# A fourth set of 32 tokens takes the way of fetched expert rows, and 384 instead of 416 stay dense

## The chip, the core and the metric

The kernel runs on one core of a Trainium2 chip. Its time is the device time of one launch in microseconds (us). Three runs of the kernel before gave 2327.8, 2332.86 and 2333.51 us; the median is 2332.86.

## What is computed

Two transformer blocks follow one another on 512 tokens of width 1024. The change lies in the last part of the first block, a feed-forward layer of 16384 experts. Every token picks 128 of them (8 heads, 16 each) and gets a gate for each pick:

```python
u_sel = u[expert]          # expert: [tokens, 128] of 16384; u, v: [16384, 1024]
v_sel = v[expert]
act = gelu(einsum('nd,ned->ne', hx, u_sel))
out = einsum('ne,ned->nd', gate * act, v_sel)
```

The sums are carried out in pairs of fp16 halves (a high and a low part), three matmuls for each product.

## The kernel before

**Two ways through the experts.** 416 tokens (`DENSE`) are computed densely: all 16384 experts in 128 chunks (`CHUNKS`) of 128. In the up pass TensorE multiplies each u tile with the tokens (`up`, 8 x 3 matmuls of 416 columns), ScalarE takes the gelu (`gelu_chunk`), and SyncE stores the result to `act_mem` (`store_act`). From chunk 58 (`AT_GATES`) on, one group of 8 tokens a chunk has its gates spread: VectorE builds one-hot rows (`pick`, four instructions), TensorE multiplies them (`spread_gates`, 16 matmuls), ScalarE copies them out (`place_gates`), and after every 13 groups (`BATCH // GROUP`) ScalarE issues one store to `gate_mem`. A batch waits for the store of the batch before the last. In the down pass SyncE loads for each chunk the v tile and the pair of `act_mem` and `gate_mem` (`load_pair`), VectorE multiplies the pair (`multiply`, L2169) and takes its low part (`low_part`, L2174), ScalarE makes the high parts, GpSimd cuts the v tile's low part (`cut_v`, L843), and TensorE does 24 matmuls of 416 columns (`down_chunk`).

**The other 96 tokens** (`FEW`, three sets of 32, `SET`) lie in the last block of 128. The 128 partitions hold a set's 32 tokens in four parts (`SIDES`), each with a quarter of the token's picks, so one fetch brings one row of u or v for each of 128 picks (512 KB), and a set takes 32 fetches of u and 32 of v. GpSimd issues them (`fetch`, L825) into six buffers (`ROWS_AHEAD`). For u, TensorE first puts the set's tokens into two PSUM banks (`turn_few`), and VectorE makes one `dot` for each row (L2013). For v, VectorE adds each row, times its weight, to the set's sum (`add_few`, L2184 and L2186), and TensorE folds the four parts at the end (L1297).

**What sets the order.** All queues are written out by hand. `dots_at` places dots 0 to 51 between the steps of VectorE's top-16 search (`CHOICE`, blocks 3, 0, 1, 2), which lasts until chunk 57 of the up pass; `dots_behind` places the others behind the picks of a group. GpSimd fetches row n before its cut of chunk `row_chunk(n)`, which is `dot_chunk(n - ROWS_AHEAD) + 4`, and waits there until dot n - 6 is done. In the down pass GpSimd and VectorE go by one rule:

```python
def fetch_chunk(k):
    return 112 * k // FEW
# GpSimd: for c in range(CHUNKS): fetch all k with fetch_chunk(k) <= c, each once add k - 6 is done; then cut_v(c)
# VectorE: for c in range(CHUNKS): multiply(c); low_part(c - 1); add all k with fetch_chunk(k) + 2 <= c
# SyncE:   for each c: load v tile c + V_LEAD (5) once cut_v(c + 1) is done; then load_pair(c) once multiply(c - 4) is done
```

The ring of v tiles has 4 places (`RING`), `pair` has 4, and the cut parts have 16. TensorE waits before the down pass until all dots are done, and before its end until all adds are.

Of the kernel before, what the change touches and what calls it, by code (L numbers as in the profile page):

```python
# [47 lines left out]
CHUNKS = 128  # L48
GROUP = 8
SET = 32  # L50
SETS = 3
FEW = SET * SETS
DENSE = S - FEW
BATCH = DENSE // 4
# [9 lines left out]
CHOICE = (3, 0, 1, 2)  # L64
FETCH = AT_ROWS + 7
STEPS = 20
FIRST_DOTS, EARLY_DOTS = 4, 52
STAIR = 65
TAIL = CHUNKS - GROUP
A_H, A_KV, A_G = 16, 4, 4  # L70
# [81 lines left out]
def build(nc, x_in, c_in, vec_in, rows1_in, rows2_in, ple_in, ada_in, w_in, u_in, v_in, u_rows_in, x_park, act_mem,  # L152
# [7 lines left out]
    with ctx:  # L160
# [3 lines left out]
        def sem(name):  # L164
            return ctx.enter_context(nc.semaphore(name))
# [253 lines left out]
        rows_used = sem("expert_rows_used")  # L419
# [52 lines left out]
        per_turn = P // GROUP  # L472

        def gate_chunk(g):

            return AT_GATES + g

        def groups_at(c):
            return [g for g in range(GROUPS) if gate_chunk(g) == c]

        def dots_behind(g):

            return [n for n in range(EARLY_DOTS, FEW)
                    if g == (n - EARLY_DOTS + 1 if n < 2 * SET else n - 2 * SET + 19)]

        def dots_at(at, step):

# [8 lines left out]

        def dot_chunk(n):

            if n >= EARLY_DOTS:
                return gate_chunk([g for g in range(GROUPS) if n in dots_behind(g)][0])  # L500
            return 19 + 7 * n // 10 if n < SET else AT_FEWER + 1 + 11 * (n - SET) // 20

        def row_chunk(n):

            return dot_chunk(n - ROWS_AHEAD) + 4
# [5 lines left out]
        def few_rows(j):  # L511

            return ps[:, 6:8, :].rearrange("p a b -> p (a b)")
# [380 lines left out]
        def _(pe):  # L894
# [11 lines left out]
            def three(out_, lhs, rhs, start, stop):  # L906

                ins = [T.matmul(out_, a, b, start=start and j == 0, stop=stop and j == 2)  # L908
                       for j, (a, b) in enumerate(((lhs[0], rhs[0]), (lhs[0], rhs[1]), (lhs[1], rhs[0])))]
                return ins[0], ins[2]  # L910
# [277 lines left out]
            def up(r, c, it):  # L1188

                pe.wait_ge(parts_ready, c + (T_EXP + 1))  # L1190
                if not (isinstance(c, int) and c < 2):
                    pe.wait_ge(gelu_ready, c - 1)
                for k in range(KC):
                    hi, lo = hr(k)
                    first, last = three(ps[:, r % 2, 0:DENSE], piece(T_EXP + r, k * P, P),
                                        (hi[:, 0:DENSE], lo[:, 0:DENSE]), k == 0, k == KC - 1)
                    if k == 0:
                        first.then_inc(begun, 1)
                last.then_inc(up_ready, 1)

            def spread_gates(r, g, first):

                pe.wait_ge(picked, g + 1)
                for q in range(2):
                    if not first:
                        pe.wait_ge(gates, g * 2 + (q - 1))
                    for t in range(4):
                        tok = q * 4 + t
                        for p in range(2):
                            mm = T.matmul(ps[:, 2 + q, t * P:(t + 1) * P], first_hot[:, r % 2, tok, :],  # L1210
                                          second_hot[:, 2 * (r % 2) + p, tok, :], start=(p == 0), stop=(p == 1))
                    mm.then_inc(gates_sum, 1)
# [9 lines left out]
            def turn_picks(i):  # L1222

                turns[0] += 1
                if i >= 2:
                    pe.wait_ge(picked, per_turn * (i - 1))
                for j in range(3):
                    mm = T.transpose(picks_of(i)[:, j * P:(j + 1) * P], chosen(i)[:, j, :], ident[:, :])
                mm.then_inc(turned, 1)

            def turn_few(j):
                first = DENSE + j * SET
                for k in range(KC):
                    for side in range(SIDES):
                        for h, half in enumerate(hr(k)):
                            mm = T.matmul(few_rows(j)[side * SET:(side + 1) * SET, k * P:(k + 1) * P],
                                          half[:, first:first + SET], ident_h, start=(h == 0), stop=(h == 1))
                mm.then_inc(few_turned, 1)
# [7 lines left out]
            for c in range(AT_FEWER // 4 * 4, CHUNKS):  # L1246
                up(c % 4, c, 0)
                if c == AT_FEWER:
                    pe.wait_ge(rows_used, SET)
                    turn_few(1)  # L1250
                if c == AT_TURN:
                    pe.wait_ge(tok_ready, 10 + NT)
                    turn_picks(0)
                    turn_picks(1)
                for g in groups_at(c):
                    spread_gates(g % 4, g, g == 0)
                    if g in (per_turn + 1, 2 * per_turn + 1):
                        turn_picks(g // per_turn + 1)
                    if g == 16:
                        pe.wait_ge(rows_used, 2 * SET)  # L1260
                        turn_few(2)


            pe.wait_ge(gelu_ready, CHUNKS)
# [26 lines left out]
            for o in range(KC):  # L1291
                for c in range(TAIL, CHUNKS):
                    lhs, rhs = down_parts(c % (2 * GROUP), o)
                    three(ps[:, o, 0:DENSE], lhs, rhs, False, c == CHUNKS - 1)
                for j in range(SETS):
                    at = DENSE + j * SET
# [67 lines left out]
        def _(act):  # L1364
# [45 lines left out]
            def attention(units, u0, parts_of):  # L1410
                def exps_of(u):
                    un = units[u]
                    soft_b, probs_b, _, sm = soft_buffers(un["kind"])
                    w = un["nc"] * P
                    act.wait_ge(max_ready, u0 + u + 1)
                    if u0 + u >= 2:
                        act.wait_ge(probs_turned, u0 + u - 1)
                    src = ps[:, 4 + u % 2, 0:w] if un["kind"] == "latent" else soft_b[:, u % 2, 0:w]
                    own.do(A.activation(probs_b[:, u % 2, 0:w], src, ACT.Exp, bias=peak(un, u),
                                        scale=1.0 if un["kind"] == "latent" else -1.0, accum_out=total(un, u)), probs)  # L1420
                    if un["kind"] == "window" and u % EIGHT == EIGHT - 1:
                        act.wait_ge(sink_shifted, u // EIGHT + 1)
                        own.do(A.activation(eight_sinks(u), eight_sinks(u), ACT.Exp), sink_exps)
# [106 lines left out]
            def bounce_in(j, dst, signal):  # L1530
                for q in range(SIDES):
                    rows = pick_mem[j][:, q * SET:(q + 1) * SET].rearrange("(s t) k -> t s k", s=SETS)
                    act.dma_start(dst[q * SET:(q + 1) * SET, :].rearrange("p (s k) -> p s k", s=SETS),
                                  rows).then_inc(signal, 16)
# [145 lines left out]
        def _(dve):  # L1680
# [322 lines left out]
            def await_rows(n):  # L2003

                dve.wait_ge(rows_fetched[n % ROWS_AHEAD], 16 * (n // ROWS_AHEAD + 1))
                return fetched_rows[:, n % ROWS_AHEAD, :]

            def dot(n):

                if n % SET == 0:  # L2010
                    dve.wait_ge(few_turned, n // SET + 1)
                row = await_rows(n)
                V.tensor_tensor_reduce(out=row, in0=row, in1=few_rows(n // SET), scale=1.0, scalar=0.0,  # L2013
                                       op0=ALU.mult, op1=ALU.add,
                                       accum_out=few_dot[:, n:n + 1]).then_inc(rows_used, 1)
# [101 lines left out]
            def take_picks(i):  # L2117

                turned_n[0] += 1
                dve.wait_ge(turned, turned_n[0])  # L2120
                src = picks_of(i)
                gate = src[:, 2 * P:3 * P].unsqueeze(2).broadcast_to([P, P, 2])
                own.settle()
                own.do(V.tensor_copy(pairs[:, 0:2, :, :].rearrange("p j n t -> p (j n) t"),
                                     src[:, 0:2 * P].unsqueeze(2).broadcast_to([P, 2 * P, 2])))
                own.link(V.tensor_scalar(pairs[:, 2, :, :], gate, GS, None, ALU.mult))
                own.link(V.scalar_tensor_tensor(out=pairs[:, 3, :, :], in0=gate, scalar=GS, in1=pairs[:, 2, :, :],
                                                op0=ALU.mult, op1=ALU.subtract))
                own.link(V.tensor_copy(src, pair_words), turned_read)
# [24 lines left out]
            for g in range(GROUPS):  # L2154
                if g % per_turn == 0:
                    take_picks(g // per_turn)
                pick(g % 2, g // per_turn, g % per_turn, g, g < 2)
                for n in dots_behind(g):
                    dot(n)


            def multiply(at, c, it):
# [260 lines left out]
```

## Time and profile before

| | |
|---|---|
| median of three runs | 2332.86 us |
| the profiled execution | 2325.09 us, its span 2323.1 us |
| TensorE busy | 2160.9 us (93% of the span) |
| VectorE, GpSimd, ScalarE busy | 1576.3, 1497.8, 920.3 us |
| up pass of the experts | about 413 to 1017 us |
| down pass | 1025 to 1577 us |
| mean granted clock of TensorE | 0.979 |
| DMA over the span | 451.55 MB, 194 GB/s |

All times in the rows are us from the span's start. Engine names there: PE is TensorE, DVE VectorE, ACT ScalarE, POOL GpSimd, SP SyncE. L2169 is line 2169 of the kernel.

### The profile page before, as it was taken

The page shows a single profiled execution, that of the slowest core. Times are in us where ns is not written, and L with a number is a line of the kernel's source. Part 1 is how long each engine was busy: PE and PEld are TensorE (multiplying, and loading weights), DVE is VectorE, ACT ScalarE, POOL GpSimd, SP SyncE. Part 2 cuts the span into 40 slices and gives each one's busy share as a digit, 9 for nine tenths or more (in the row PEclk, how much of TensorE's full clock was granted, in tenths as well). Part 3 has the DMA queues.
Part 4 walks back from the last instruction along what each step waited for, and adds up shares of the span by engine and source line. Part 5 has one row for each costly group of instructions (what it writes and reads, how often), then busy time and mean ns, then how long its engine had stood idle before and what let it go on. Part 6 is the DMA issues. An engine that isn't in the chain of part 4 may idle for free. (4 is left out here: it accounts for less than half of the span.)

```text
span 2323.1 us, 36974 instructions
## 1 busy us (share of the span) xinstructions
PE 2160.9 (93%) x12908; PEld 1182.5 (51%) x12908; DVE 1576.3 (68%) x2807; ACT 920.3 (40%) x1606; POOL 1497.8 (64%) x1032
## 2 busy tenths in 40 slices
PE   5998898999989999989999999998988979989897
PEld 2543543555546666545555555553555435446543
DVE  7597866998896677038889888953047454556644
ACT  2211411455556666543333333322156222245522
POOL 6885586768755555467787777753844758733473
PEclk9999998999999999999999999999999999989998
DMA  7333543579978999989999999852300223300031
GB/s 281 101 96 115 187 148 118 159 266 350 333 237 268 290 355 341 286 312 337 332 341 337 329 338 326 286 182 61 113 29 1 89 75 99 93 19 1 13 91 42
DMA packets 218057, 451.55 MB, mean 194 GB/s; under 512 B 83200, under 2 KB 132544, under 8 KB 217920
## 3 DMA queue, kind: packets, MB, share of 16 engines
q1 hardware_dynamic: 119696, 313.67, 39.7%
q0 software_dynamic: 27648, 100.68, 12.2%
q10 hardware_dynamic: 70576, 35.40, 6.2%
q8 instruction: 83, 1.36, 0.2%
q14 instruction: 54, 0.44, 0.1%
HBM read 390.86 MB, written 58.82 MB: 194 GB/s over the span
## 5 line engine op out<-in xcount | busy, mean ns | idle before, releaser
L908 PE MATMUL ps<-hT,parts 128*128 128x416 f16 (+1 forms) x4800 | 932.9, 355 | 30.6 <-POOL parts L811 9.8
L908 PEld LDWEIGHTS ps<-hT,parts 128*128 128x128 f16 x4800 | 467.2, 98 | 475.7 <-issue 21.7
L908 PE MATMUL ps<-arena 128*128 128x416 f16 x3072 | 544.3, 340 | 12.8 <-DVE arena L2174 11.3
L908 PEld LDWEIGHTS ps<-arena 128*128 128x128 f16 x3072 | 300.7, 98 | 254.2 <-issue 15.0
L817 POOL TENSOR_TENSOR parts<-ring,parts 128x1024 f16<-128x1024 f32 x120 | 256.0, 2135 | 198.4 <-ACT ring L1541 197.2
L808 POOL TENSOR_SCALAR parts<-ring 128x1024 f16<-128x1024 f32 x141 | 163.5, 1160 | 240.0 <-PE ps L908 205.7
L811 POOL TENSOR_TENSOR parts<-ring,parts 128x1024 f16<-128x1024 f32 x141 | 309.7, 2196 | 11.8
L843 POOL TENSOR_TENSOR arena<-ring,arena 128x1024 f16<-128x1024 f32 x128 | 293.5, 2303 | 24.9 <-ACT arena L1578 22.9
L2169 DVE TENSOR_TENSOR route<-arena 128x416 f32<-128x416 f32 x128 | 169.9, 1327 | 128.0 <-DMA arena<-gate_mem 125.1
L1375 ACT ACTIVATE arena<-ps 128x512 f32<-128x512 f32 (+9 forms) x266 | 135.9, 532 | 246.8 <-PE ps L908 141.7
L908 PE MATMUL ps<-arena,parts 128*128 128x512 f16 x876 | 193.5, 381 | 11.6 <-POOL parts L811 5.8
L1593 ACT ACTIVATE arena<-route 128x416 f16<-128x416 f32 x128 | 70.3, 549 | 318.5 <-DVE route L2169 318.5
L2186 DVE SCALAR_TENSOR_TENSOR hT<-arena,spare,hT 128x1024 f32<-128x1024 f32 x93 | 193.9, 2085 | 0.0
L825 POOL DMA_INDIRECT arena<-v,spare x96 | 108.6, 1131 | 97.0 <-DVE hT L2186 84.8
L852 POOL TENSOR_SCALAR arena<-arena 128x512 f16<-128x512 f32 (+3 forms) x80 | 43.9, 549 | 191.0 <-ACT arena L1375 191.0
L1520 ACT ACTIVATE spare<-ps 128x416 f32<-128x416 f32 x128 | 66.3, 518 | 251.2 <-PE ps L908 249.2
L809 POOL TENSOR_SCALAR ring<-ring 128x1024 f32<-128x1024 f32 x141 | 161.3, 1144 | 0.0
L908 PEld LDWEIGHTS ps<-arena,parts 128*128 128x128 f16 x876 | 85.4, 98 | 119.4 <-issue 12.6
L1578 ACT ACTIVATE arena<-ring 128x1024 f16<-128x1024 f32 x128 | 133.2, 1041 | 11.8 <-DMA ring<-v 11.8
L1540 ACT ACTIVATE parts<-ring 128x1024 f16<-128x1024 f32 x120 | 125.8, 1048 | 2.7 <-DVE xT L2108 2.7
L2013 DVE CUSTOM_DVE_ANT_0 arena<-arena,ps 128x1024 f32<-128x1024 f32 x96 | 115.9, 1216 | 14.7 <-DMA arena<-u_rows,spare 8.4
L1541 ACT ACTIVATE ring<-ring 128x1024 f32<-128x1024 f32 x120 | 125.6, 1046 | 0.0
(223 smaller groups left out, 2628.4 us busy)
## 6 DMA issues: line engine op xcount, KB each, us to landing
ring<-w SPq DMA_DIRECT2D x133, 512.0 KB, 3.6
ring<-u SPq DMA_DIRECT2D x128, 512.0 KB, 6.2
ring<-v SPq DMA_DIRECT2D x128, 512.0 KB, 4.6
act_mem<-spare SPq DMA_DIRECT2D x128, 208.0 KB, 5.1
gate_mem<-arena ACTq DMA_DIRECT2D x4, 6656.0 KB, 51.4
arena<-act_mem SPq DMA_DIRECT2D x128, 208.0 KB, 4.2
arena<-gate_mem SPq DMA_DIRECT2D x128, 208.0 KB, 5.5
arena<-ada_w SPq DMA_DIRECT2D x48, 512.0 KB, 5.3
```

What stands on the lines that cost most here:

```text
L808: G.tensor_scalar(dst[:, 0, :], src, WS, 1.0, ALU.mult, ALU.mult).then_inc(scaled, 1)
L809: G.tensor_scalar(src, src, WS, 1.0, ALU.mult, ALU.mult).then_inc(scaled, 1)
L811: G.tensor_tensor(dst[:, 1, :], src, dst[:, 0, :], ALU.subtract).then_inc(parts_ready, 1)
L817: G.tensor_tensor(dst[:, 1, :], src, dst[:, 0, :], ALU.subtract).then_inc(parts_ready, 1)
L843: G.tensor_tensor(dst[:, 1, :], src, dst[:, 0, :], ALU.subtract).then_inc(parts_ready, 1)
L908: ins = [T.matmul(out_, a, b, start=start and j == 0, stop=stop and j == 2) for j, (a, b) in enumerate(((lhs[0], rhs[0]), (lhs[0], rhs[1]) ...
L1375: return A.activation(dst, src, ACT.Copy, scale=scale)
L1540: A.activation(parts[:, n % RING, 0, :], src, ACT.Copy, scale=WS).then_inc(raised, 1)
L1541: A.activation(src, src, ACT.Copy, scale=WS).then_inc(raised, 1)
L1578: A.activation(v_parts[:, c % (2 * GROUP), 0, :], ring[:, (S_V + c) % RING, :], ACT.Copy).then_inc(v_high, 1)
L2169: V.tensor_tensor(prod[:, at % 2, :], pair[:, at % 4, 0, :], pair[:, at % 4, 1, :], ALU.mult).then_inc(product, 1)
L2186: V.scalar_tensor_tensor(out=sums, in0=row, scalar=w, in1=sums, op0=ALU.mult, op1=ALU.add).then_inc(rows_used, 1)
```

## The change

The number of sets goes from 3 to 4, so 128 tokens (the whole last block) go by fetched rows and 384 stay dense. All sizes that hang on it follow: matmuls, gelus, multiplies and stores have 384 columns, there are 48 groups of gates instead of 52 in batches of 12 instead of 13 groups, 128 fetches, dots and adds instead of 96 on each side, and `fetch_chunk` spreads 128 fetches over the same 112 chunks. The third set's dots stand behind the gates of groups 18 to 46. The dots of the fourth set come on VectorE after the last group; TensorE turns that set's tokens after chunk 108 (`AT_LAST`), and for the fetches its dots count two to a chunk from chunk 109.

```diff
-SETS = 3
+SETS = 4
-FIRST_DOTS, EARLY_DOTS = 4, 52
+FIRST_DOTS, EARLY_DOTS, AT_LAST = 4, 52, 108
@@ dots_behind
             return [n for n in range(EARLY_DOTS, FEW)
-                    if g == (n - EARLY_DOTS + 1 if n < 2 * SET else n - 2 * SET + 19)]
+                    if g == (n - EARLY_DOTS + 1 if n < 2 * SET else 18 + 29 * (n - 2 * SET) // SET) and n < 3 * SET]
@@ dot_chunk
+            if n >= 3 * SET:
+                return AT_LAST + 1 + (n - 3 * SET) // 2
@@ TensorE, up pass
-                    if g in (per_turn + 1, 2 * per_turn + 1):
+                    if g == per_turn + 1:
                         turn_picks(g // per_turn + 1)
                     if g == 16:
                         pe.wait_ge(rows_used, 2 * SET)
                         turn_few(2)
+                if c == AT_LAST:
+                    pe.wait_ge(rows_used, 3 * SET)
+                    turn_few(3)
@@ VectorE, after the groups
+            for n in range(3 * SET, FEW):
+                dot(n)
```

## Rows read from the trace of the kernel before

**Rows 1.** Windows: engine busy (instructions), then granted clock, DMA share, GB/s.

```profile
820.00:880.00 60.00, 60.00 (x475) 38.29 (x474) 44.99 (x74) 38.90 (x58) 36.49 (x24) 1.00 1.08 355
...
1200.00:1400.00 200.00, 200.00 (x1139) 111.29 (x1138) 181.10 (x138) 71.85 (x96) 155.38 (x89) 1.00 0.93 332
```

**Rows 2.** Timeline of one chunk with gates: start, us, engine, line.

```profile
858.91 4.38 PE L908 MATMUL ps<-hT,parts 128*128 128x416 f16 x24
...
859.11 0.69 DVE L2146 TENSOR_TENSOR xT<-xT,ps 128x1024 f16<-128x1024 f16 x1 [1.30 <-PE ps L1210]
...
861.70 1.21 DVE L2013 CUSTOM_DVE_ANT_0 arena<-arena,ps 128x1024 f32<-128x1024 f32 x1
...
864.02 4.38 PE L908 MATMUL ps<-hT,parts 128*128 128x416 f16 x24
```

**Rows 3.** Timeline of TensorE before the gates: turn_few, and the wait of chunk 57.

```profile
481.06 1.09 PE L1236 MATMUL ps<-xT,hT 128*32 128x128 f16 x64
...
670.75 1.54 PE L1228 MATMUL ps<-ident,arena 128*128 128x128 f32 x6 [2.88 <-DVE xT L2108]
```

**Rows 4.** Pieces of the chain that ended last, in the down pass.

```profile
1373.94 2.14 POOL arena L843
...
1377.26 6.24 DMA arena<-gate_mem
...
1389.07 0.76 issue
1389.82 1.02 POOL arena L825
```

**Rows 5.** Waits from 1040 to 1500 us: total, times, longest.

```profile
POOL arena L825 <- DVE hT L2186: 84.8, 37, 3.0
```

**Rows 6.** Timeline of VectorE in the down pass.

```profile
1301.46 0.58 DVE L2169 TENSOR_TENSOR route<-arena 128x416 f32<-128x416 f32 x1
...
1302.46 1.27 DVE L2186 SCALAR_TENSOR_TENSOR hT<-arena,spare,hT 128x1024 f32<-128x1024 f32 x1
...
1304.66 3.15 DVE L2186 SCALAR_TENSOR_TENSOR hT<-arena,spare,hT 128x1024 f32<-128x1024 f32 x1
...
1333.94 3.15 DVE L2186 SCALAR_TENSOR_TENSOR hT<-arena,spare,hT 128x1024 f32<-128x1024 f32 x1
```

**Rows 7.** Waits from 480 to 640 us, VectorE's.

```profile
DVE arena L2013 <- DMA arena<-u_rows,spare: 8.4, 10, 1.7
DVE arena L2013 <- PE ps L1236: 5.9, 1, 5.9
```

**Rows 8.** The four gate stores (L1571): time to landing.

```profile
DMA to landing us min/median/max: 43.5/51.4/61.9
```

**Rows 9.** Timeline of GpSimd with two fetches a chunk.

```profile
611.40 0.95 POOL L825 DMA_INDIRECT arena<-u_rows,spare  x1
...
615.91 0.95 POOL L825 DMA_INDIRECT arena<-u_rows,spare  x1 [0.16 <-issue]
```

**Rows 10.** Timeline of the down pass: start, chunk 3, no gap from 1064.55, end.

```profile
1025.28 10.41 PE L908 MATMUL ps<-arena 128*128 128x416 f16 x48 [8.44 <-DVE arena L2174]
...
1032.39 2.51 DVE L2169 TENSOR_TENSOR route<-arena 128x416 f32<-128x416 f32 x1
...
1064.55 473.09 PE L908 MATMUL ps<-arena 128*128 128x416 f16 x2688 [1.05 <-DVE arena L2174]
...
1567.69 4.38 PE L908 MATMUL ps<-arena 128*128 128x416 f16 x24
...
1572.50 4.38 PE L908 MATMUL ps<-arena 128*128 128x416 f16 x24
```

**Rows 11.** The gate half of the pair (L756): time to landing.

```profile
DMA to landing us min/median/max: 2.6/5.5/7.9
```

**Rows 12.** DMA issues from 1503 to 1532 us, where no rows are fetched.

```profile
arena<-gate_mem SPq DMA_DIRECT2D x11, 208.0 KB, 4.4
```

**Rows 13.** Windows behind the change of pass, columns as in rows 1.

```profile
1020.00:1030.00 10.00, 4.72 (x17) 2.23 (x18) 6.40 (x4) 1.89 (x3) 4.89 (x4) 0.66 1.03 411
```

## The prediction

> **What bounds the kernel now.** I read the windows first, to see which engine has no gaps in which stage. In the second half of the experts (the "down" pass) TensorE is busy all the time: 1139 matmuls in 200 us, 0.1756 us each, so a chunk of 24 takes 4.21 us [rows 1]. That is 416 columns at the granted clock of 1.00 with about 2.4 ns on top, so with 384 columns a matmul takes 0.1625 us and a chunk 3.90 us. In the "up" pass a chunk that also spreads gates takes 5.11 us between two starts of its matmuls [rows 2], so TensorE sets the pace there too. Read no further, and the change gives 0.31 us on each of 256 chunks.
>
> But TensorE is not alone. Before chunk 57 it waits for VectorE's gates [rows 3]. And in the down pass the chain of waits runs for long stretches not through TensorE but round a loop [rows 4]: VectorE adds a fetched row; 0.80 us later GpSimd issues the next fetch (1.02 us), then cuts a v tile (2.14 us); SyncE then issues that tile's successor and, behind it, the pair of act_mem and gate_mem (1.18 us from the cut's end to the gate issue); the pair lands 6.24 us later; then VectorE can multiply. GpSimd waited for VectorE's adds 84.8 us in 37 places [rows 5]. The reader is to see that this loop is near the bound before anything is changed: VectorE's seven chunks take 1333.94 - 1304.66 = 29.28 us against TensorE's 7 x 4.21 = 29.5 [rows 6].
>
> **The up pass.** (1) Chunks 0 to 57. VectorE sets the end. Its own waits there are 8.4 us for rows whose fetch is paced by TensorE's chunks, and 5.9 for turn_few(1) at chunk 43, which comes 44 x 0.31 = 13.8 us earlier [rows 7]. Together 14.3 can go, no more, though TensorE saves 18; I take -13, and keep -6 if rows are just as late. (2) Gates: 52 x 5.11 = 265.7 becomes 48 x (5.11 - 0.31) = 230.4, -35.3. Chunks without gates: 18 x 4.21 = 75.8 becomes 22 x 3.90 = 85.8, +10. turn_few(3) is 64 matmuls, which took 1.09 us before [rows 3], +1.1. The picks on VectorE (four fewer) and its 32 more dots of 1.3 us lie beside TensorE: a chunk of 4.80 holds 2.6 of picks and 1.3 of dot [rows 2], and they cost nothing until they pass 4.80. (3) The gate stores: one takes 43.5 to 61.9 us [rows 8], and the batch after next waits for it. A batch now lasts 12 x 4.80 = 57.6 us instead of 66.4, with more rows fetched beside it, so the one at 61.9 is late: +4 (0 to 8). (4) The last set. Rows 102 to 127 are fetched two to a chunk. Where the kernel does that now, GpSimd needs 615.91 - 611.40 = 4.51 us a chunk for two issues and a cut [rows 9], against TensorE's 3.90: 13 x 0.61 = 7.9, less some 3 of lead. The last gate store runs beside; the DMA engines are at 355 GB/s in the window where a store and one row a chunk meet [rows 1]. Two a chunk and the store ask for more. I take +8 (3 to 18). ScalarE's larger pick transfers are hidden: pick_row is ready before chunk 12. Sum of the up pass: -13 - 35.3 + 10 + 1.1 + 4 + 8 = -25 (-38 to -8). The change of pass, 8.44 us of waiting now [rows 10], has 6 row fetches behind the last dots: +2 (0 to 8).
>
> **The down pass, where it is decided.** Rows ahead are 6, and k's fetch stands before chunk fc(k) = 112k//FEW on GpSimd, its add in chunk fc(k)+2 on VectorE. Fetch k waits for add k-6. With FEW = 96, fc(k-6) = fc(k) - 7, so the cut of chunk c waits for VectorE's chunk c-5. With FEW = 128 six rows are only 5.25 chunks: the cut of c waits for VectorE's chunk c-3, and for c-4 in one of seven. The pair of chunk c is issued behind the cut of c+1. Write M(c) for the multiply's start, A(c) for the end of that chunk's adds, K for the way from an add to the multiply. Now M(c) >= A(c-4) + K; after, M(c) >= A(c-2) + K, and A(c-3) + K in one of seven. All that waits behind GpSimd's fetch is late with it: the cut, SyncE's v load, and behind that the pair.
>
> K from the chain [rows 4]: 0.80 + 1.02 + 2.16 + 1.18 + landing. The gate piece's landing is 6.24 in the chain, 5.5 in the median, 2.6 at the least, and 4.4 where no rows are fetched (1503 to 1532 us) [rows 11, 12]. The traffic will be slower than now, since the loop itself is; I take 5.0, so K = 10.2, and keep 4.4 and 6.24 (9.6 and 11.4). A(c) - M(c) is three instructions of VectorE, 1.00 for the two short ones and 1.2 [rows 6], 2.2 us (384 columns save 0.03 on each of two), and 3.4 where two rows are added.
>
> The lags repeat every seven chunks, and the dearest way round goes 5, 2, 0 and back to 5: steps of 3, 2 and 2 chunks. So seven chunks take at least 3K + 2.2 + 2.2 + 3.4 = 30.6 + 7.8 = 38.4 us. After the chunk with two adds GpSimd still has the cut before to finish when its row is free, 2.2 more (0 to 2.2): 40.6, or 5.8 a chunk, against TensorE's 27.3. The low end is 28.8 + 7.8 = 36.6, the high one 34.2 + 10 = 44.2.
>
> Now from chunk 3's multiply at 1032.39 to the last fold at 1577.3 is 545 us [rows 10]. After: chunks 3 to 9 some 30 us, then 105 chunks, 15 x 40.6 = 609, then TensorE alone: 15 x 3.90 = 58.5, one us before it, and eight folds of 0.8 instead of 0.6 (four sets instead of three): 66. Sum 705, +160.
>
> Total: -25 + 2 + 160 = +137. The profiled execution took 2325.1 (span 2323.1), so 2462 against its own time; it lies below all three runs, 7.8 under their median of 2332.9, and I set the sum on the median: 2470. The runs spread over 5.7 us, so 0.3%, 7 us, is about what this measurement can tell from no change.
>
> **Rivals.**
> *Only the shared access bounds.* VectorE's adds and multiplies and GpSimd's cuts take turns: an add that takes 1.27 alone takes 3.15 beside a cut [rows 6]. Seven chunks are 7 cuts of 2.14 [rows 4] and 14 x 0.5 + 6 x 1.2 = 14.2, in all 29.2, near the 29.28 found. After: 15.0 + 6.5 + 9.6 + 0.1 = 31.2, below 40.6. Were the window of rows no bound, the down pass would be 30 + 15 x 31.2 + 66 = 564, +19, and the whole -4: 2329. For it: the sum fits so well. Against: it leaves K out, which the chain shows. 0.07.
> *Short landings.* All pairs land in the 2.6 us of the least row: K = 7.8, cycle 23.4 + 10 = 33.4, down 597, +52, whole +29: 2362. Against: the median is 5.5. 0.06. The Trainium skill, DMA: Bandwidth & Descriptors, "Anatomy of one DMA", gives 2.0 us plus the bytes over 436 GB/s for a GpSimd-issued transfer; for 197 KB that would be an estimate of 2.45 us, and the whole would be about +24. The trace's median of 5.5, issued by SyncE behind a v tile, speaks against it.
> *TensorE stays the bound (faster).* Then the down pass gives 128 x 0.31 = 40 back, less 1.6 of folds: -61, 2272. It needs K + 2.2 <= 2 x 3.90, so K below 5.6, of which 5.2 is spent before the landing. For it: TensorE has no gap now from 1064.55 on [rows 10]. 0.04.
> *TensorE's clock.* It will be idle a third of each down chunk. After the 8.44 us of waiting its granted clock was 0.66 over 10 us in which it was busy for 4.7; in the 200 us with no gap it was 1.00 [rows 1, 13]. At its lower level, 1.2 GHz, a chunk is 7.7 us: were it there all the time, +197 on top. But it would then be busy throughout and climb again. 0.03, over 2535. The Trainium skill, TensorE: Matmul & The Clock Gate, Part 1, says an idle array falls to the half clock; whether gaps this short do it, no row of this stage shows.
>
> **How the numbers follow.** The forecast has 0.80. Its own range is 2398 (cycle 36.6, -60, and up pass -13 more) to 2535 (cycle 44.2, +54, and up +17 more, not both in full). The 80% range is the same, 2395 to 2535; it leaves out the cases at 2272, 2329, 2362 and the clock, 0.2. Faster by over 0.3%: the 0.04 and a third of the 0.07; same: another third; slower: the rest, 0.91.
>
> **What would show it.** In the profile after: chunks of 3.90 in the up pass; chunk 57 waiting longer for VectorE; seven down chunks in 37 to 44 us on VectorE; TensorE at 65 to 70% there; waits of VectorE for gate_mem several hundred us in total, in nearly each chunk; GpSimd waiting for VectorE's adds in nearly each; GB/s near 260 instead of 332. The prediction is wrong if GpSimd's fetches seldom wait for adds, or if landings are near 2.6 us.

## The result and the profile after

The changed kernel takes 2539.41 us (median of 4 runs, 2535.31 to 2542.95) against 2333.19 for the kernel before (4 runs, 2327.8 to 2334.63): a ratio of 1.0886, 95% interval 1.0866 to 1.0907, so 8.9% slower. The forecast was 2470 and the range 2395 to 2535; the direction and the stage were as forecast, the size was not: the result lies 4 us above the range. The profiled execution has a span of 2537.1 us, 214.0 more than before. The page's part 1 now gives TensorE 2155.8 us busy, 85% of the span, VectorE 1513.0, GpSimd 1545.7; the mean granted clock is 0.946.

In the kernel after, L910 is the dense matmul, L2176 the multiply, L2181 the low part, L2191 and L2193 the adds, L827 the fetch, L845 the cut of a v tile, L693, L757 and L758 SyncE's issues of the v tile, act_mem and gate_mem.

The windows that answer to [rows 1], and the whole down pass (columns as there):

```profile
820.00:880.00 60.00, 60.00 (x508) 40.73 (x507) 47.19 (x78) 42.29 (x63) 39.23 (x27) 1.00 1.08 379
1060.00:1750.00 690.00, 501.52 (x2688) 275.90 (x2688) 343.25 (x357) 169.40 (x232) 382.96 (x233) 0.90 0.73 243
1200.00:1400.00 200.00, 140.27 (x757) 76.26 (x758) 105.55 (x103) 48.52 (x66) 105.86 (x69) 0.92 0.74 244
```

With gates TensorE still has no gap. In the down pass it does 757 matmuls in 200 us where it did 1139; no engine is near full, and the DMA engines moved 244 GB/s where they moved 332.

TensorE's timeline at the first gates, near the end of the up pass, and at the change of pass:

```profile
659.13 1.17 PE L1230 MATMUL ps<-ident,arena 128*128 128x128 f32 x6 [3.19 <-DVE xT L2113]
...
671.11 4.06 PE L910 MATMUL ps<-hT,parts 128*128 128x384 f16 x24
...
675.90 4.06 PE L910 MATMUL ps<-hT,parts 128*128 128x384 f16 x24
...
942.01 4.07 PE L910 MATMUL ps<-hT,parts 128*128 128x384 f16 x24 [0.77 <-POOL parts L819]
946.53 4.07 PE L910 MATMUL ps<-hT,parts 128*128 128x384 f16 x24 [0.44 <-POOL parts L819]
...
1004.53 9.52 PE L910 MATMUL ps<-arena 128*128 128x384 f16 x48 [18.80 <-DVE arena L2181]
```

A chunk with gates is 675.90 - 671.11 = 4.79 us (5.11 before, [rows 2]), one with two fetches 946.53 - 942.01 = 4.52. The up pass ends at 1004.53 - 18.80 = 985.73; before it was 1025.28 - 8.44 = 1016.84 [rows 10]. So the up pass gave 31.1 us, and the wait behind it took back 10.4. ScalarE's timeline says what was late there:

```profile
992.34 2.00 ACT L1583 ACTIVATE arena<-ring 128x1024 f16<-128x1024 f32 x2 [8.89 <-DMA gate_mem<-arena]
```

That is the last gate store. The trace's rows of gate_mem (the four stores, and the landing of all transfers with that name):

```profile
L1576 ACTq DMA_DIRECT2D gate_mem<-arena x4: 378/393/437, 721.7 to 895.7; - x4
...
DMA to landing us min/median/max: 2.5/5.0/96.5
```

Issued at 895.7, it landed 96.5 us later, at 992.2; before, the longest took 61.9 [rows 8]. It shares the DMA engines with two row fetches a chunk: from 935 to 955 us they moved 409 GB/s at a share of 1.04. SyncE's queue holds the first pairs behind this store, and behind the pairs a store of act_mem, for which ScalarE's last gelu waited another 8.35 us, until 1002.69. From the first down matmul to chunk 3's multiply is 7.8 us (7.1 before); from there to the last fold 779.2 us (544.9). So -31.1 + 10.4 + 0.7 + 234.3 = +214.3, the whole difference of the spans. TensorE's timeline of the end of the down pass and VectorE's of its chunk 3:

```profile
1752.30 5.49 PE L910 MATMUL ps<-arena 128*128 128x384 f16 x24 [6.65 <-POOL parts L813]
...
1790.61 0.97 PE L1302 MATMUL ps<-spare,hT 128*128 128x32 f32 x8
```

```profile
1012.36 0.55 DVE L2176 TENSOR_TENSOR route<-arena 128x384 f32<-128x384 f32 x1
```

The waits from 1010 to 1750 us (total, times, longest), the answer to [rows 5], and the issue line of the pair's gate half with its median landing in us, to [rows 11]:

```profile
DVE route L2176 <- DMA arena<-gate_mem: 365.6, 78, 10.7
POOL arena L827 <- DVE hT L2193: 276.4, 70, 7.4
PE ps L910 <- DVE arena L2181: 200.0, 66, 7.8
```

```profile
arena<-gate_mem SPq DMA_DIRECT2D x124, 192.0 KB, 5.0
```

Each engine of the loop waits for the next one round: VectorE for the pair, GpSimd for VectorE's add; TensorE, which is not in the loop, waits for VectorE. That is the loop of the prediction, and the median landing is the 5.0 us taken there.

One turn of it on VectorE, on GpSimd, and the first issues on SyncE's queue:

```profile
1409.25 1.28 DVE L2193 SCALAR_TENSOR_TENSOR hT<-arena,spare,hT 128x1024 f32<-128x1024 f32 x1
...
1411.51 4.34 DVE L2193 SCALAR_TENSOR_TENSOR hT<-arena,spare,hT 128x1024 f32<-128x1024 f32 x2
1422.04 0.56 DVE L2176 TENSOR_TENSOR route<-arena 128x384 f32<-128x384 f32 x1 [6.19 <-DMA arena<-gate_mem]
...
1426.86 0.56 DVE L2176 TENSOR_TENSOR route<-arena 128x384 f32<-128x384 f32 x1 [2.60 <-DMA arena<-gate_mem]
...
1439.63 0.56 DVE L2176 TENSOR_TENSOR route<-arena 128x384 f32<-128x384 f32 x1 [8.28 <-DMA arena<-gate_mem]
...
1453.12 0.56 DVE L2176 TENSOR_TENSOR route<-arena 128x384 f32<-128x384 f32 x1 [8.98 <-DMA arena<-gate_mem]
```

```profile
1411.34 1.08 POOL L827 DMA_INDIRECT arena<-v,spare  x1 [6.22 <-DVE hT L2193]
1412.44 2.33 POOL L845 TENSOR_TENSOR arena<-ring,arena 128x1024 f16<-128x1024 f32 x1
1414.92 1.76 POOL L827 DMA_INDIRECT arena<-v,spare  x1 [0.15 <-issue]
1416.70 2.13 POOL L845 TENSOR_TENSOR arena<-ring,arena 128x1024 f16<-128x1024 f32 x1
```

```profile
1419.00 0.33 SPq L693 DMA_DIRECT2D ring<-v  x1
...
1420.02 0.35 SPq L758 DMA_DIRECT2D arena<-gate_mem  x1
```

An add ends at 1409.25 + 1.28 = 1410.53. The fetch that waited for its row starts at 1411.34 and a cut follows it; but the pair for the multiply at 1426.86 stands behind the next cut, and between the two is another fetch. So this step is 1426.86 - 1410.53 = 16.33 us and not K, the prediction's 10.2 us from the end of an add to the multiply that it allows. Of the 6.1 us more, GpSimd has 4.3 (its second cut ends at 1418.83, 8.30 after the add, where K has 3.98), and the pair's landing 1.8 (6.84 us from 1420.02). The next two steps are plain: the add behind that multiply ends 2.23 later, and 10.54 on is the multiply at 1439.63; 2.22 later its add ends, and 11.27 on is the multiply at 1453.12. The three steps and three times 2.22 are 44.8 us, and that is the price of seven chunks: over 99 chunks it is 631.2 us, 6.38 a chunk, 44.6 for seven. Before, over the same chunks, it was 29.6. The turn is a usual one: over the 14 rounds of these chunks the three steps are 17.0 (16.0 to 19.2), 10.2 and 10.4 us in the mean.

### The profile page after: what moved, and what is told of

Same layout as the page of the kernel before. It is cut to its first block and busy times, and to the rows that moved or that the text cites. A ratio compares the mean times of both kernels' runs of the same rounds, so it can differ in the third digit from the quotient of the medians.

```text
span 2537.1 us, 37220 instructions
## 1 busy us (share of the span) xinstructions
PE 2155.8 (85%) x12921; PEld 1197.5 (47%) x12921; DVE 1513.0 (60%) x2883; ACT 909.8 (36%) x1598; POOL 1545.7 (61%) x1096
## 5 line engine op out<-in xcount | busy, mean ns | idle before, releaser
L910 PE MATMUL ps<-hT,parts 128*128 128x384 f16 (+1 forms) x4800 | 894.3, 347 | 38.2 <-POOL parts L819 13.4
L910 PE MATMUL ps<-arena 128*128 128x384 f16 x3072 | 575.1, 352 | 225.5 <-DVE arena L2181 218.8
L910 PEld LDWEIGHTS ps<-hT,parts 128*128 128x128 f16 x4800 | 466.7, 98 | 447.8 <-issue 25.5
L910 PEld LDWEIGHTS ps<-arena 128*128 128x128 f16 x3072 | 315.9, 105 | 482.7 <-DVE arena L2181 191.5
L2176 DVE TENSOR_TENSOR route<-arena 128x384 f32<-128x384 f32 x128 | 104.4, 816 | 384.6 <-DMA arena<-gate_mem 380.4
L827 POOL DMA_INDIRECT arena<-v,spare x128 | 136.7, 1068 | 307.4 <-DVE hT L2193 276.4
L845 POOL TENSOR_TENSOR arena<-ring,arena 128x1024 f16<-128x1024 f32 x128 | 283.1, 2215 | 35.3 <-ACT arena L1583 33.2
L1598 ACT ACTIVATE arena<-route 128x384 f16<-128x384 f32 x128 | 66.8, 522 | 550.2 <-DVE route L2176 550.1
L910 PE MATMUL ps<-arena,parts 128*128 128x512 f16 x876 | 194.0, 382 | 11.6 <-POOL parts L813 5.8
L2193 DVE SCALAR_TENSOR_TENSOR hT<-arena,spare,hT 128x1024 f32<-128x1024 f32 x124 | 193.1, 1557 | 1.7
L2018 DVE CUSTOM_DVE_ANT_0 arena<-arena,ps 128x1024 f32<-128x1024 f32 x128 | 153.9, 1215 | 58.4 <-DMA arena<-u_rows,spare 37.8
L1525 ACT ACTIVATE spare<-ps 128x384 f32<-128x384 f32 x128 | 62.9, 491 | 234.5 <-PE ps L910 186.8
L827 POOL DMA_INDIRECT arena<-u_rows,spare x128 | 121.7, 951 | 37.8 <-issue 18.3
L910 PEld LDWEIGHTS ps<-arena,parts 128*128 128x128 f16 x876 | 85.6, 99 | 119.7 <-issue 13.4
```

Of the source, the lines that this page charges most:

```text
L827: G.indirect_dma_start(out=fetched_rows[:, n % ROWS_AHEAD, :], out_offset=None, in_=rows, in_offset=bass.IndirectOffsetOnAxis(ap=few_idx[: ...
L845: G.tensor_tensor(dst[:, 1, :], src, dst[:, 0, :], ALU.subtract).then_inc(parts_ready, 1)
L2193: V.scalar_tensor_tensor(out=sums, in0=row, scalar=w, in1=sums, op0=ALU.mult, op1=ALU.add).then_inc(rows_used, 1)
```

## The experiments

The theory: the down pass goes at the pace of the loop fetch, cut, pair, multiply, add, which is set by how many chunks lie between the add that frees a row and the multiply that waits behind it; 128 fetched tokens cut that lag from four chunks to two (three in one of seven). The rivals: VectorE and GpSimd taking turns; the bytes of the fetched rows; TensorE's clock. Seven chunks are given below by the multiplies' starts from chunk 9 to chunk 108. Each ratio is taken to runs of the kernel before made beside that kernel (medians 2329.9 to 2330.3 us, 2333.2 for the one after); "less" in the text is against the 2539.4 of the kernel after, where nothing else is said. A kernel with one run has no interval; the runs of one kernel spread over 17 us at most.

| kernel | us, median | ratio to before (95%) | seven chunks |
|---|---|---|---|
| before | 2333.2 | | 29.6 |
| after | 2539.4 | 1.0866 to 1.0907 | 44.6 |
| seven row buffers | 2419.3 | 1.0337 to 1.0436 | 36.1 |
| pair ahead of the v tile | 2412.9 | 1.0304 to 1.0405 | 35.8 |
| adds a chunk sooner | 2402.9 (one run) | | 35.6 |
| both of the first two | 2351.0 | 1.0072 to 1.0123 | 31.9 |
| all three | 2343.7 | 1.0037 to 1.0080 | 31.9 |
| half-width rows | 2500.2 (one run) | | 42.1 |
| half-width adds | 2495.4 (one run) | | 41.3 |
| before, four row buffers | 2672.7 (one run) | | 52.1 |
| v cut by VectorE | 2298.9 | 0.9830 to 0.9884 | 28.8 |
| the same, pair first | 2274.1 | 0.9735 to 0.9779 | 26.8 |
| before, v cut by VectorE | 2324.2 | 0.9957 to 0.9982 | (TensorE's) 29.5 |

**Seven row buffers.**

```diff
-ROWS_AHEAD = 6
+ROWS_AHEAD = 7
```

> The changed kernel with seven row buffers in place of six, nothing else. Theory (the window of rows sets the down pass): seven rows are 6.1 chunks of fetches in place of 5.25, so the cut of chunk c waits for VectorE's chunk c-4 and the multiply for A(c-3)+K. From the steps measured in the changed kernel (16.3, 10.5 and 11.3 us from the end of an add to the multiply it allows, 2.2 us more each for the adds, a mean of 15) seven chunks take 7/3 x 15 = 35 us, and not under the 31.2 of VectorE and GpSimd taking turns. So the down pass between chunks 9 and 108 falls from 6.38 us a chunk to 4.5 to 5.0: 135 to 185 us less, 2355 to 2405 us in all. VectorE's waits for gate_mem fall from 380 us to under 200. Rival, shared access: the instructions are the same, 6.38 us a chunk stay, 2539 +- 15. Rival, DMA bandwidth or TensorE's clock: no change in bytes or in matmuls, 2539 +- 15.

2419.3 us, 120 less, all of it between chunks 9 and 108 (510.7 us for 631.2): seven chunks fell to 36.1. The steps are a little longer than the 15 us assumed (36.1 / (7/3) = 15.5), so a chunk is 5.16 us and not at most 5.0, and the whole ended 14 us above its range. The waits from 1060 to 1430 us (in the kernel after, from 1060 to 1440, they were 162.7 and 191.3 us in total):

```profile
POOL arena L827 <- DVE hT L2193: 108.5, 46, 2.9
DVE route L2176 <- DMA arena<-gate_mem: 88.4, 40, 5.6
```

Neither an instruction nor a byte was taken away, so shared access, bandwidth or the clock as the bound of the kernel after are out.

**The pair ahead of the v tile.**

```diff
                 for r in range(4):
-                    load(S_V + V_LEAD + r, tile_of(v_in, it * 4 + (V_LEAD + r)), it)
                     load_pair(r, it * 4 + r, False)
+                    load(S_V + V_LEAD + r, tile_of(v_in, it * 4 + (V_LEAD + r)), it)
```

(and the same in the last chunks)

> The changed kernel with SyncE issuing the pair of chunk c ahead of the v tile that it now issues first. Theory: the v tile's buffer comes free with the cut of chunk c+1, so the pair waits for that cut; ahead of it, it waits for the cut of c alone, one chunk sooner. M(c) >= A(c-3)+K as with seven rows: 31.2 to 35 us for seven chunks in place of 44.6, 135 to 200 us less, 2340 to 2405 us in all, if no other wait takes its place. SyncE's own wait ahead of the pair is then for the product of an earlier chunk. Rivals (shared access, DMA bandwidth, clock): 2539 +- 15, since the same transfers and instructions are done.

2412.9 us, 127 less, 35.8 for seven: the same chunk of lag, gained at another place of the loop, is worth the same. It ended 8 us above its range.

**Each add one chunk sooner.**

```diff
-                while k < FEW and fetch_chunk(k) + 2 <= c:
+                while k < FEW and max(2, fetch_chunk(k) + 1) <= c:
```

> The changed kernel with each add placed one chunk sooner on VectorE, in the chunk after its fetch in place of the second after it. Six row buffers, order of issues unchanged. Theory: the cut of chunk c then waits for A(c-4) in place of A(c-3), the multiply for A(c-3)+K, as with seven rows: 36 us for seven chunks, 2415 +- 15, unless the row has not landed when its add is due (a fetched row lands 5.5 us after its issue in the median, and a chunk is 5.2): then VectorE waits for rows, some 1 to 2 us in most chunks, and it ends between, 2430 to 2500. Rivals (bandwidth, clock, instructions): 2539.

2402.9 us in one run, 35.6 for seven, inside the range. A third place, the same price. From 1060 to 1440 us none of its larger waits is VectorE's for a row: they had landed.

**The kernel before with four row buffers.**

```diff
-ROWS_AHEAD = 6
+ROWS_AHEAD = 4
```

> The kernel before, 96 fetched tokens and 416 dense, with four row buffers in place of six. Theory: four rows are 4.67 chunks of fetches in place of 7, so the multiply of chunk c waits for A(c-2) or A(c-1) in place of A(c-4): seven chunks in 3.5 to 4.2 steps of 12.4 us, 43 to 52 us in place of 29.3, so 200 to 340 us more in the down pass, and some more in the up pass, where the dots use the same buffers: 2530 to 2720 us, with the dense work and the number of fetches of the kernel before. Rival, shared access or bandwidth: 2333 +- 20, since neither the adds nor the bytes change.

2672.7 us, 342 more than the kernel before, with its dense work and its 96 fetches. Seven chunks take 52.1 us, the high end of what was expected. So the lag by itself, without the fourth set, does what the change did, and more. Its waits from 1060 to 1440 us have the same form:

```profile
DVE route L2169 <- DMA arena<-gate_mem: 235.7, 47, 11.6
POOL arena L825 <- DVE hT L2186: 208.8, 39, 9.3
```

**Rows of half the width.**

```diff
+                wide = D if n < FEW else D // 2
-                rows = ... else v_in.rearrange("c p n -> (c p) n")
+                rows = ... else v_in.rearrange("c p (h n) -> (c p h) n", h=2)
-                    out=fetched_rows[:, n % ROWS_AHEAD, :], ...
+                    out=fetched_rows[:, n % ROWS_AHEAD, 0:wide], ...
```

> The changed kernel with the v rows fetched at half their width (256 KB each in place of 512 KB); the other half of each buffer keeps older data, so the sums of the few tokens are not the reference's. All else is unchanged. Theory (the loop through the row buffers): the bytes are not what binds. What can shrink is the landing of the pair of act_mem and gate_mem, from 5.0 us toward 4.0; three steps for seven chunks make 3 us, 45 us in all: 2480 to 2539. Rival, DMA bandwidth (fetched rows crowd the queues): the down pass moves 128 x 256 KB = 33 MB less, at the 240 GB/s measured there 137 us less: 2400.

2500.2 us, 39 less, where the bandwidth rival asked for 137. Seven chunks lost 2.5 us, near the 3 of three shorter landings: the multiplies that waited for their pair started 3.8 us behind its issue in the median, 5.25 in the kernel after. The window from 1060 to 1440 us shows how little the DMA engines had to do:

```profile
1060.00:1440.00 380.00, 269.03 (x1513) 147.75 (x1512) 236.57 (x199) 92.76 (x126) 210.91 (x137) 0.96 0.64 203
```

**Adds of half the width.**

```diff
                 w, sums = few_dot[:, k:k + 1], few_sum(k // SET)
+                if k % SET:
+                    row, sums = row[:, 0:D // 2], sums[:, 0:D // 2]
```

> The changed kernel with 124 of the 128 adds of the few tokens done over 512 of the 1024 columns; the other half of their sums is left out, so the output is not the reference's. Six row buffers and the order of issues as in the changed kernel. Theory: three steps with some four adds set the seven chunks; each add is 0.6 us shorter alone and up to 1.6 shorter where it shares access with a cut, and less of the 2.2 to 6 us of queueing remains: 37.5 to 42 us in place of 44.6, 2435 to 2500 us. If the extra 4 us over the forecast of 40.6 come from the shared access of the adds and the cuts, it ends under 40 (under 2470); if they come only from two cuts in a row on GpSimd, near 42 (2500).

2495.4 us, 44 less, 41.3 for seven, between the two marks and nearer to that of the two cuts. An add alone takes 0.74 us here in place of 1.27, so three on the way are 1.6 of the 3.3 gained. The pair also lands in 4.4 us in the median in place of 5.0, three times 0.6, which is all the rest. But the run doesn't divide the 4 us above the forecast. An add of half the width that meets a cut (here the one from 1311.03) still takes long:

```profile
1310.57 3.15 DVE L2195 SCALAR_TENSOR_TENSOR hT<-arena,spare,hT 128x512 f32<-128x512 f32 x1
```

So the time spent on the shared access fell little, and how much of those 4 us it costs stays open.

**Both loosenings, and all three.** The edits are those above, together.

> Both loosenings at once: seven row buffers, and the pair of chunk c issued ahead of the v tile. Theory: each alone gave one chunk (44.6 us for seven chunks became 36.1 and 35.8), together the multiply waits for A(c-4)+K, as in the kernel before. Steps of 15 to 15.5 us over four chunks would allow seven chunks in 27, so the loop no longer binds, and what does is VectorE and GpSimd taking turns: 31.2 us for seven chunks, 4.46 a chunk; some 70 to 75 us less than either alone, 2335 to 2350 us. If instead a rival bounds what is left at 36 (the DMA engines, now at a share of 0.87 at 293 GB/s, or TensorE's clock), 2410 to 2420.

> All three loosenings: seven row buffers, the pair ahead of the v tile, adds one chunk sooner. Theory: with the first two the loop already lies beyond the bound of the shared access, so a third chunk brings nothing: within 10 us of the kernel with the first two, 2335 to 2350; slower than it if VectorE then waits for rows that have not landed. If the loop still binds there, this one is faster by 10 us or more.

2351.0 and 2343.7 us, as expected, the first within 1 us of its range. The third loosening is within 10 us of the two: the loop no longer binds. VectorE's timeline of the kernel with all three shows what does:

```profile
1295.41 5.07 DVE L2193 SCALAR_TENSOR_TENSOR hT<-arena,spare,hT 128x1024 f32<-128x1024 f32 x2
1300.39 0.55 DVE L2176 TENSOR_TENSOR route<-arena 128x384 f32<-128x384 f32 x1
1300.86 3.01 DVE L2181 TENSOR_TENSOR arena<-route,arena 128x384 f16<-128x384 f32 x1
1303.80 1.27 DVE L2193 SCALAR_TENSOR_TENSOR hT<-arena,spare,hT 128x1024 f32<-128x1024 f32 x1
...
1307.13 2.48 DVE L2176 TENSOR_TENSOR route<-arena 128x384 f32<-128x384 f32 x1
```

It has no gap, and its window from 1020 to 1540 us gives VectorE 512.94 busy of 520.00; but a low part takes 0.55 us at one place (1290.87) and 3.01 at another (1300.86), where GpSimd's cut of 2.13 us runs from 1301.32. Seven chunks are 31.3 to 31.9 us all the way; the prediction's sum for taking turns was 31.2. The Trainium skill, SBUF — State Buffer, "Terms", has the port pair of VectorE and GpSimd as an exclusive lock held for a whole instruction; the 3.01 agrees, being about the 0.55 and the 2.13 together.

**The v tiles cut by VectorE.** If these two explanations hold, one edit takes away both: the cut leaves GpSimd, so it stands neither behind a fetch nor in VectorE's way.

```diff
             for c in range(CHUNKS):
                 while n < 2 * FEW and fetch_chunk(n - FEW) <= c:
                     fetch(n)
                     n += 1
-                cut_v(c)
+            pool.wait_ge(parts_ready, S_V + CHUNKS)
...
+            def cut_v(c):
+                dve.wait_ge(v_high, c + 1)
+                src, dst = ring[:, (S_V + c) % RING, :], v_parts[:, c % (2 * GROUP), :, :]
+                V.tensor_tensor(dst[:, 1, :], src, dst[:, 0, :], ALU.subtract).then_inc(parts_ready, 1)
+
+            dve.wait_ge(parts_ready, S_V)
+            cut_v(0)
+            cut_v(1)
+            cuts = 2
...
                     add_few(k)
                     k += 1
+                while cuts < min(2 + 2 * c, c + 5, CHUNKS):
+                    cut_v(cuts)
+                    cuts += 1
```

> The changed kernel (128 fetched tokens, six row buffers, order of issues as it was) with the low parts of the v tiles cut by VectorE in place of GpSimd, four chunks ahead of their use; GpSimd then does nothing but fetches in the down pass. Theory: the cut no longer stands behind a fetch that waits for an add, so the pair's way leaves the loop; and VectorE no longer takes turns with a 2.14 us cut. VectorE's own work for seven chunks is 7 x (0.47 + 0.47 + 1.15 for a cut of 1024 columns, estimated from the adds' 1.2) + 8 x 1.2 = 24.2 us, under TensorE's 7 x 3.90 = 27.3. So the down pass runs at 3.9 to 4.1 us a chunk, 6.38 before; against the changed kernel 225 to 245 us less for 99 chunks and some 10 at its start and end: 2280 to 2315, faster than the kernel before by 1 to 2%. Rival, another bound at 31.8 us for seven chunks (the DMA engines at 330 GB/s): 2340 to 2350, as the kernel with both loosenings. Rival: VectorE, with the cuts added, waits for the row fetches or for ScalarE's high parts in turn and becomes the bound: over 4.5 us a chunk, 2350 and more.

> The same, with the pair issued ahead of the v tile as well. Theory: the pair's way is already clear with a lead of three chunks (9.7 us against some 7 for issue and landing), so this changes the time by less than 5 us. If the pairs still arrive late in the kernel without it, this one is faster by 10 us or more.

2298.9 us with six row buffers, 1.4% faster than the kernel before and 241 us faster than the one after, from moving one instruction a chunk to another queue (and up to four chunks ahead). With the pair first it is 2274.1, 2.4% faster than before. That the second edit would bring less than 5 us was a miss: it brought 25. The lag of three chunks must hold not only issue and landing (1.2 and, from 1259.71 to 1266.66 us, 6.9) but also the 3.4 us of VectorE between a multiply and the cut behind it: 11.5 us in three chunks, 3.84 a chunk, with nothing to spare for a chunk with two adds or a later landing; measured are 28.8 / 7 = 4.12. That this is the reason is worked out from one turn and not tested apart. The window from 1020 to 1440 us, a wait in it and VectorE's timeline, of the kernel with the pair first:

```profile
1020.00:1440.00 420.00, 414.98 (x2546) 249.17 (x2545) 383.81 (x456) 173.25 (x223) 146.91 (x121) 1.00 1.03 397
```

```profile
DVE route L2170 <- DMA arena<-gate_mem: 21.9, 30, 1.4
```

```profile
1310.08 0.56 DVE L2170 TENSOR_TENSOR route<-arena 128x384 f32<-128x384 f32 x1 [0.25 <-issue]
1310.55 0.55 DVE L2175 TENSOR_TENSOR arena<-route,arena 128x384 f16<-128x384 f32 x1
1311.02 1.28 DVE L2187 SCALAR_TENSOR_TENSOR hT<-arena,spare,hT 128x1024 f32<-128x1024 f32 x1
1312.22 1.22 DVE L2193 TENSOR_TENSOR arena<-ring,arena 128x1024 f16<-128x1024 f32 x1
```

No instruction of VectorE is drawn out any more, a chunk is 1313.74 - 1310.08 = 3.66 us at this place, and TensorE is busy for 415 of 420 us at a granted clock of 1.00. This is the kernel that the change's own arithmetic asked for: the forecast of the rival with TensorE as the bound was 2272. That it comes so near is in part luck, since TensorE waits 18.35 us at the change of pass here, where the rival's sum had 8.44 + 2.

**The kernel before, v cut by VectorE.** The same edit on the kernel before.

> The kernel before (96 fetched, 416 dense) with the low parts of the v tiles cut by VectorE. Theory: seven chunks were 29.3 us there, both by the shared access (29.2) and by TensorE's 416 columns (29.5); taking away the first leaves the second: within 5 us of the kernel before, 2325 to 2338. If the kernel before was in truth held by the shared access or the loop, it gains 10 us or more.

2324.2 us, ratio 0.9969: 6 us less than the kernel before, one more than the 5 allowed, and half of what would speak for another bound. TensorE is busy for all of the 380 us from 1060 to 1440, and did 1140 matmuls from 1200 to 1400, as many as before: it is the bound there, so a looser loop could give this kernel nothing. So the gain of vector_cuts_first over the kernel before, 50 us more than this, comes from the 384 dense tokens once the loop and the shared access are out of the way.

## Why the prediction was right in kind and short in size

- **Up pass, forecast -25, measured -31.1.** The wait at chunk 57 ends at 659.13 in place of 670.75: -11.6 for -13. VectorE's two waits of [rows 7] fell to 0.7 and 0.5 us:

```profile
DVE arena L2018 <- DMA arena<-u_rows,spare: 0.7, 2, 0.4
DVE arena L2018 <- PE ps L1238: 0.5, 1, 0.5
```

  A gate chunk came to 4.79, as worked out. The two stalls were set too high: no batch waited for a gate store (+4 forecast), and the tail with two fetches a chunk cost some 4 us, not 8; its pace of 4.51 was right (4.52), the lead was longer. The range "-38 to -8" is not what the ends of its terms add up to, which is -36 to -4; the result lies in both.
- **Change of pass, forecast +2, measured +10.4.** The last gate store was costed only for what it takes from the tail. It took 96.5 us beside two fetches a chunk, and the next stage waits for it, the pairs in SyncE's queue and ScalarE's high parts both. No run takes the fetches away from beside it, so that they are the reason for the 96.5 is argued and not tested. The stall forecast for the up pass came here.
- **Down pass, forecast +160, measured +234.** The lags, the links of the loop and K were right: in one plain turn (add's end 1304.20, multiply 1314.37) K was 10.17 for 10.2. Chunks 3 to 9 took 45 us in place of 30: the prediction let the loop begin only behind them, and it was there from the start. The seven chunks took 44.6 us, not 40.6, and this is the step that failed: "After the chunk with two adds GpSimd still has the cut before to finish when its row is free, 2.2 more (0 to 2.2)". It is a term in the right place, and mis-sized: the step with three chunks of lag took 16.33 us, 6.1 over K, since it holds a whole second cut and a fetch of 1.76 drawn out beside two adds (4.3), and a landing of 6.8 where 5.0 was taken (1.8). The other two steps were 0.3 and 1.1 over K. The dearest way was also another than the forecast one: not by chunks 5, 2 and 0 of each seven but by 4, 1 and 6, so the chunk with two adds (3.4) lay beside it, 1.2 less: 6.1 + 0.3 + 1.1 - 1.2 - 2.2 = 4.1. Over 99 chunks that is 57 us; with 15 at the start and 2 at the end, the 74 missing.
- **The range.** Its high end took the cycle of 44.2 in full, and 44.6 came; the change of pass was given 8 at most, and 10.4 came; the 30 for chunks 3 to 9 had no range, and 45 came. All three went one way, the up pass alone went the other.
- **The rivals.** Shared access alone would have given 2329; it wasn't the bound here, but it is the bound of the kernel with both loosenings, which took 31.9 us for the 31.2 forecast. Short landings did not come: the median is 5.0. (By the same sum a landing of 2.45 us gives +22, not the prediction's +24.) The clock fell only to 0.90 in the down pass (1.00 before), with TensorE waiting for VectorE and not the other way; where the waits were gone it was 1.00 again.

## What to carry to other kernels

When a stage looks bound by one engine, divide the buffers by their use per step: the lag in steps between freeing a buffer and the work queued behind its refill is what a loop of fixed length K is divided by, and a third more fetches took two of its four steps. Cost such a loop not by its clean turns but with everything else that stands in the same queue between two of its links. And before the lag is loosened, ask whether the instruction in the loop must stand behind the waiting one at all: one more buffer gave back 120 us, moving the cut to another engine's queue 241.

## What the runs showed of the hardware

- In the fastest kernel the DMA engines moved 397 GB/s for 420 us from memory into SBUF (166.82 MB), at a share of 1.03. The Trainium skill, DMA: Bandwidth & Descriptors, "Where 436 GB/s comes from", gives some 358 GB/s as the limit of memory for a core, half of what a stack of it yields to its two cores; the measurement, of one core at work, is 11% above it.
- The same cut of 1024 columns takes 2.13 us on GpSimd and 1.22 on VectorE, and on GpSimd it also holds up VectorE's instruction beside it by 2.4 us or so (3.01 for 0.55). With the cuts on VectorE no instruction of VectorE in the window from 1020 to 1440 us was drawn out: an add took 1.27 to 1.28 us in all places.
